# Product-key choices that read their scores from PSUM, one step sooner, with the turns of x at other steps

## The reference, cut to what matters

```python
q = (xb @ wq).reshape(PEER_BLOCK, PEER_HEADS, 2, D_KEY_HALF)
s1 = jnp.einsum('thd,hnd->thn', q[:, :, 0], keys1)
s2 = jnp.einsum('thd,hnd->thn', q[:, :, 1], keys2)
v1, i1 = lax.top_k(s1, PEER_TOPK)
v2, i2 = lax.top_k(s2, PEER_TOPK)
cand = (v1[..., :, None] + v2[..., None, :]).reshape(...)
cidx = (i1[..., :, None] * N_KEYS + i2[..., None, :]).reshape(...)
top_s, sel = lax.top_k(cand, PEER_TOPK)
eidx = jnp.take_along_axis(cidx, sel, axis=-1)
gate = jax.nn.softmax(top_s.astype(jnp.float32), axis=-1).astype(xb.dtype)
act = jax.nn.gelu(jnp.einsum('td,thkd->thk', xb, u_tab[eidx]))
return jnp.einsum('thk,thkd->td', gate * act, v_tab[eidx])
```

## Time and profile before

| | |
|---|---|
| median of three runs | 3038.26 us (3035.58 to 3039.6) |
| the profiled execution's own time | 3035.47 us |
| its span in the profile | 3033.6 us |
| mean granted TensorE clock | 0.846 of 2.4 GHz |
| busy: TensorE, VectorE, ScalarE, GpSimd | 2303.3, 2067.1, 2044.8, 1228.0 us |
| bytes moved, mean | 1226.64 MB, 404 GB/s |
| of these by the gathers' queue | 1107.36 MB, 88.6% of the DMA engines' span |

### The profile page before, as it was taken

How to read it: one execution, slowest core, us unless ns; L and a number is a source line. 1 busy time by engine, 2 the same in 40 slices (tenths; PEclk the granted TensorE clock), 3 DMA queues, 4 the chain that set the end, 5 groups by cost and what they waited for, 6 DMA issues and landing times.

```text
span 3033.6 us, 36636 instructions
## 1 busy us (share of the span) xinstructions
PE 2303.3 (76%) x12800; PEld 1880.0 (62%) x12800; DVE 2067.1 (68%) x5112; ACT 2044.8 (67%) x3704; POOL 1228.0 (40%) x1060
## 2 busy tenths in 40 slices
PE   9976887787668887877777877888777766667666
PEld 7765776665557766656566665665556555555555
DVE  2466887566688775666888744566588899955454
ACT  1277666668677566776677666667767777676666
POOL 0133333334333333444443344433344445456653
PEclk9987989998889889987887998989888886666666
DMA  7599999999999999999999999999999999999998
GB/s 301 190 416 397 413 408 414 419 420 413 420 421 409 420 417 415 420 404 420 420 416 406 404 422 419 419 419 396 405 420 420 418 418 409 415 418 419 422 420 333
DMA packets 180568, 1226.64 MB, mean 404 GB/s; under 512 B 20736, under 2 KB 21952, under 8 KB 40736
## 3 DMA queue, kind: packets, MB, share of 16 engines
q0 software_dynamic: 152064, 1107.36, 88.6%
q1 hardware_dynamic: 28032, 116.88, 9.6%
q10 hardware_dynamic: 288, 0.07, 0.0%
HBM read 1219.37 MB, written 4.86 MB: 404 GB/s over the span
## 4 chain that ended last, share of the span: by engine, by line
DMA 35%; DVE 24%; PE 22%; ACT 13%; issue 5%; POOL 1%; DVEq 0%; POOLq 0%; ACTq 0%
DMA ring<-in_uv,idx 35%; DVE ring L1459 12%; PE expert_sum L1116 8%; ACT ring L873 5%; PE mm L914 4%; PE x_ps L976 3%; ACT weights L869 2%; PE mm L1038 2%; PE mm L923 2%; ACT L860 1%; DVE pairs_left L1306 1%; ACT dots L860 1%; DVE pairs_left L1394 1%; DVE top_i L1315 1%; DVE pick_f L1400 1%
## 5 line engine op out<-in xcount | busy, mean ns | idle before, releaser
L661 POOL DMA_INDIRECT ring<-in_uv,idx x1056 | 1227.7, 1163 | 1781.8 <-PE expert_sum L1116 1574.7
L1116 PE MATMUL expert_sum<-ident_sb,ring 128*128 128x128 f32 x8448 | 1367.1, 317 | 581.3 <-ACT ring L873 579.8
L1459 DVE CUSTOM_DVE_ANT_0 ring<-ring,xn 128x1024 f32<-128x1024 f32 x1056 | 1286.7, 1223 | 737.8 <-DMA ring<-in_uv,idx 730.2
L1116 PEld LDWEIGHTS expert_sum<-ident_sb,ring 128*128 128x128 f32 x8448 | 1150.5, 165 | 838.6 <-ACT ring L873 767.9
L873 ACT ACTIVATE ring<-ring,weights 128x1024 f32<-128x1024 f32 x1056 | 1213.2, 1149 | 34.3
L860 ACT ACTIVATE dots<-dots 128x1 f32<-128x1 f32 x1056 | 211.5, 200 | 771.6 <-DVE dots L1459 768.2
L869 ACT ACTIVATE weights<-dots,gate 128x1 f32<-128x1 f32 x1056 | 311.1, 295 | 38.2
L914 PE MATMUL mm<-stream,xn_in 128*128 128x256 f32 (+1 forms) x912 | 258.4, 421 | 71.9 <-ACT qkvg L708 56.3
L1038 PE MATMUL mm<-turn,stream 128*128 128x256 f32 (+2 forms) x1024 | 278.4, 401 | 2.8 <-DVE xn_in L1155 2.8
L914 PEld LDWEIGHTS mm<-stream,xn_in 128*128 128x128 f32 (+1 forms) x912 | 166.9, 199 | 113.7 <-ACT qkvg L708 66.0
L923 PE MATMUL mm<-xn_in,stream 128*128 128x256 f32 (+1 forms) x640 | 183.7, 426 | 34.8 <-ACT conv_tmp L699 22.6
(11 more groups left out here) (233 smaller groups left out, 1517.4 us busy)
## 6 DMA issues: line engine op xcount, KB each, us to landing
stream<-in_wq SPq DMA_DIRECT2D x36, 1024.0 KB, 12.0
stream<-in_w_ret SPq DMA_DIRECT2D x26, 1024.0 KB, 9.4
stream<-in_w_conv SPq DMA_DIRECT2D x24, 1024.0 KB, 11.9
ring<-in_uv,idx POOLq DMA_INDIRECT x1056, 12.3
ring<-in_w_ret SPq DMA_DIRECT2D x7, 1024.0 KB, 12.4
x<-in_x SPq DMA_DIRECT2D x8, 512.0 KB, 8.7
w_out_sb<-in_w_out SPq DMA_DIRECT2D x1, 4096.0 KB, 28.9
out_y<-xn SPq DMA_DIRECT2D x8, 512.0 KB, 11.9
```

The costliest lines, as they stand in the source:

```text
L661: pool.indirect_dma_start(ring[:, g % RING, :], None, uv, bass.IndirectOffsetOnAxis(ap=rows, axis=0)).then_inc(landed[g % RING], 16)
L1116: ins = pe.matmul(expert_sum[:, c * P:(c + 1) * P], ring[:, g % RING, D + c * P:D + (c + 1) * P], ident_sb[:, :], is_transpose=True, start ...
L1459: dve.tensor_tensor_reduce(u, u, xn[:, t % 3, :], 1.0, 0.0, ALU.mult, ALU.add, dots[:, g % RING:g % RING + 1]).then_inc(dotted, 1)
```

## The change

The copies of the prompt tiles' scores to SBUF are taken out, with the tensor `scores`. VectorE's choice reads the scores in `tp`, and waits for TensorE's products (`keyed`) in place of the copies. Only the sample tile's scores are still copied, at the slot at which tile 7's scores of the same head would have been. `choose_at` is one slot sooner for every choice but one: head 1 of tile 0 stays at slot 0. `scores_left_tp` waits until VectorE has read the scores (`scores_read`, counted after the second half's MATCH_REPLACE8) and the sample's are copied. The turns of x move: tile 3 from slot 58 to 61, tile 5 from 274 to 277, sample from 526 to 528, tile 6 from 530 to 531, tile 7 from 534 to 537.

```diff
@@ x_turn_at
-    return first_use_at(group_of(t)) - 10 + 4 * place(t)
+    if group_of(t) == len(GROUPS) - 1:
+        return first_use_at(group_of(t)) + [-8, -5, 1][place(t)]
+    return first_use_at(group_of(t)) - 10 + 7 * place(t)
@@ choose_at
-    return choose_at(PH - 1, t - 1) + 7 * (h + 1) if t == SAMPLE else scores_at(h, t) + 1
+    return choose_at(PH - 1, t - 1) + 7 * (h + 1) if t == SAMPLE else scores_at(h, t)
@@ layer_kernel
-        scores = sb("scores", [P, 2, NK])
...
             if t < SAMPLE:
-                return scores[:, :, :]
+                return tp[:, score(h, t) % 2, 0:2 * NK].rearrange("p (s k) -> p s k", s=2)
@@ score_copies (ScalarE)
-                    if c == 0:
+                    if t < SAMPLE:
                         continue
                     n = rows_of(t)
-                    yield scores_at(h, t)
+                    yield scores_at(h, t - 1)
                     act.wait_ge(keyed, c)
-                    if t < SAMPLE:
-                        wait(act, scores_read, pick(h, t) - 1)
@@ scores_left_tp (TensorE)
                 if n:
                     pe.wait_ge(first_read, 2)
-                wait(pe, keyed_copied, n - 1)
+                sample = sum(t == SAMPLE for _, t in SCORES[:n])
+                wait(pe, scores_read, n - 1 - sample)
+                wait(pe, keyed_copied, sample)
@@ choices (VectorE)
-                            if s == 0:
-                                dve.wait_ge(keyed_copied, c)
+                            if s == 0 and t < SAMPLE:
+                                dve.wait_ge(keyed, c)
+                            elif s == 0:
+                                dve.wait_ge(keyed_copied, h + 1)
```

## The result

The changed kernel takes 3042.64 us (median of 10 runs, 3035.08 to 3049.46), the kernel before 3036.84 us (10 runs): a ratio of 1.0019, with a 95% interval of 1.0011 to 1.0027. A second set gave 3041.14 against 3037.37 us, 1.0013 (1.0003 to 1.0022). It is slower by 4 to 6 us: at the edge of what was called 0.2%, but a ratio of 1 lies outside both intervals. The time lies inside the stated range, and its direction is wrong: a gain of 0.9 us was forecast.

What follows compares the result with a forecast made beforehand. The gathers' DMA bytes were taken to bound the kernel. Terms of -1.4 (waits), 0 (indices), 0 (PSUM reads) and +0.5 us (turns) summed to -0.9, so 3038.26 us became 3037.4, range 3030 to 3044 us.

Steps and rivals of the forecast that it cites:

- The bound: Long plain stretch: the gathers' bytes set the pace, DMA share 1.01, about 2.5 us a slot, no compute engine full.
- The copies and the waits for them: ScalarE's 63 score copies: removal worth 0; VectorE's 52.2 us of waits for them: gain 1.4 us, between 0 and 4.2.
- Each choice starts one slot sooner: VectorE's choices, with exponential and gates, come one slot sooner; one worse wait, at slot 34, at most 0.4 us, taken as 0.
- rival (c): Tiles 0 and 1: VectorE blocks before unwritten scores, 14 waits, 35 us, a third may pass: +12 us, 3050 us; chance 0.08.
- The 3%: Share of a stall reaching the DMA engines, about 3%, read from GpSimd's late gathers near 442 and 909 us.
- The turns of x: Moved turns meet scores due at TensorE: 7.8 us more waiting, 0.2 us at 3%, taken as 0.5 us lost.
- Reading PSUM: VectorE's 378 reads of scores from PSUM: 6 ns more each, 2.3 us under DMA time, counted as 0.
- The earlier indices: GpSimd's one wait for a choice's indices in the loop, 3.46 us, mostly goes, worth 0.
- The signs: Observations set as proof of being right, among them VectorE's L1303 wait below 20 us and dips summing to 5 to 8 us.
- The sign set for being wrong: A DMA loss of over 2 us at slots 50 to 100, or in the 20 us after a moved turn.

Runs made afterwards that it cites:

- all choices late: Changed kernel with every choice one slot later, where it was before the change: 3036.78 us against 3036.82 for the kernel before, ratio 1.0004.
- turns alone: Kernel before with only the turns of x moved as in the change, copies and choices kept: 3043.12 us against 3036.82, ratio 1.0017.
- the scores sooner: Changed kernel with query passes of tiles 0, 1 and turns of tiles 2, 3 one slot sooner: 3039.65 us against 3037.37 for the kernel before, ratio 1.001.
- tiles 0 and 1 late: Changed kernel with only the choices of tiles 0 and 1 one slot later: 3038.77 us, ratio 1.0004 to the kernel before.

## Why the prediction was wrong, point by point

- **The bound.** Right: the DMA share is 1.01 in plain stretches in both kernels, and no engine became the bound.
- **The copies and the waits for them.** The sign was right and the size too small. 1.4 us was taken, between 0 and 4.2; all choices late against turns alone says -6.3 us by the medians and -3.9 by the ratios. So the upper bound was too low or just reached; it counted only what windows of 20 us lacked in DMA share.
- **"Each choice starts one slot sooner", at no price.** This is the step that failed. It was costed at nothing because a wait of VectorE passes on 3%, and for only one choice was a wait foreseen, at slot 34 (it came: 3.46 us). The same arithmetic (is TensorE's product there when VectorE reaches it?) was not made for the twelve choices from slot 51 on. The earlier trace rows was read as ScalarE's lateness, TensorE having "long been done". That is so at slot 52, but not everywhere: the copies' own row has 10.0 us of idle time that ended with TensorE's scores. One such copy, behind VectorE's wait of 3.21 us at slot 87 of the kernel before:

```profile
384.75 0.38 ACT L806 ACTIVATE scores<-tp 128x256 f32<-128x256 f32 x1 [3.22 <-PE tp L1066]
```

  In the busy stretch of tiles 0 and 1 TensorE is up to three slots late, and the copy's slot was part of the margin that hid it. Measured: 24.7 us more waits by the means in slots 30 to 130 (28.2 to 31.0 against 3.9 to 7.0), and 4.2 us (medians) to 6.0 us (rows) more time. This is rival (c), which was given 35 us of waits, a third passed on and a chance of 0.08; its waits are the ones that the runs show, at half its price or less. That the loss comes with the early choices of tiles 0 and 1 is shown; that it comes through their waits alone is not, by the run with the scores sooner.
- **The 3%.** It was taken from two gaps of GpSimd which fell, by the prediction's own argument, when other transfers filled the DMA engines, and used as a rule. If the waits of tiles 0 and 1 are the whole cause, the runs give a sixth to a quarter for waits that follow each other every seven slots (4.2 to 6.0 of 24.7 us); and a stretch with a stall of 14.54 us and two smaller gaps grew by 11.0 us.
- **The turns of x.** 0.5 us was taken of 7.8. Measured +6.3 us with copies (2.9 for tile 3's, 3.2 for the others), and by the medians 3.8 for the others without copies. So this term was too small as well. But the forecast waits don't explain it. In the profile after, TensorE waits 0.84 us before tile 5's score at 278 and not at all before the one at 539, where 4.1 and 3.6 us were forecast. In the run with the turns alone, which has the loss, they are 2.75 and 0.51 us; with all choices late, which has no loss, the first is 4.60 us and the second isn't there. The two rows at slot 278:

```profile
936.19 1.15 PE L1068 MATMUL tp<-keys_sb,qT 128*128 128x128 f32 x4 [2.75 <-issue]
```

```profile
932.33 0.98 PE L1068 MATMUL tp<-keys_sb,qT 128*128 128x128 f32 x3 [4.60 <-issue]
```

  Which wait makes the moved turns dearer is open. One thing that the profile shows is argued only: ScalarE's part of the norm, with its two table loads, has moved with the turn, and TensorE waits 4.57 us for ScalarE at 928.67. Against it: with tiles 0 and 1 late the same wait lasts 4.58 us, in a kernel without a clear loss.
- **Reading PSUM.** Right: MATCH_REPLACE8 takes 280 ns from tp against 276, and FIND_INDEX8 291 (lines below). The measured 4 to 6 ns decide against the 65 ns more that were worked out from the page of the Trainium skill (Perfetto Trace Analysis, Optimizing Scalar/DVE Operations).
- **The earlier indices.** Right: GpSimd's wait for the indices of gather 32, 3.46 us, is gone. The profile after puts one other wait down to indices, 2.69 us at 399.44 before gather 96. The indices written just before it are those of a choice of tile 1, which that gather doesn't use, so the name of that wait isn't its cause.
- **The signs.** VectorE's wait at the choices was to fall below 20 us and is 36.8; the dips were to sum to 5 to 8 us and sum to 11.6. The sign set for being wrong, over 2 us of DMA time lost at slots 50 to 100, was just reached (2.0 us in the window at 300, around slot 61) and not passed, so it was set too high for a loss that is spread.

The tile view of tp in the changed kernel (duration min/median/max in ns):

```profile
L1305 DVE MAX8 top_v<-tp x126: 279/295/300, 127.8 to 2512.3; 128x8 f32<-128x128 f32 x126
...
L1307 DVE FIND_INDEX8 top_i<-top_v,tp x126: 289/291/293, 128.2 to 2512.7; 128x8 uint32<-128x128 f32 x126
...
L1308 DVE MATCH_REPLACE8 pairs_left<-top_v,tp x126: 278/280/284, 128.5 to 2513.0; 128x128 f32<-128x128 f32 x126
```

In all, by the medians and in this order: moved turns +6.3, reading from PSUM -6.3, early choices +4.8 (the mean of the two sets, against all choices late). By the ratios and the other pairs of runs they are 5 to 6, 4 to 6 and 3 to 5 us. They were forecast as +0.5, -1.4 and 0. The sizes are those of this order of steps; another was measured only in part (the turns other than tile 3's cost 3.8 us by the medians without the copies, 3.2 with them).

## What to carry to other kernels

When a copy between two engines is taken out, look at how late the producer is in each stretch, and not only at how late the copier was: the copy's step may be the margin that covers the producer, and a consumer that works in order then blocks its own main work in front of it. Here the early choices with two slots behind their scores (tiles 2 to 7) cost nothing that could be measured, and those with one slot (tiles 0 and 1 from slot 51 on) came with a loss of 3 to 5 us. And don't turn one observed gap into a rate for how much of a stall reaches the bounding resource: measure a stall where nothing else fills in. Where a change has several parts, as here, run each alone: two of them cost and one gained, and the sum hid that.

## What the hardware showed that was not expected

The DMA share doesn't see all that is lost. Slots 32 to 160, changed kernel and the one with tiles 0 and 1 late (stretches):

```profile
219.00:608.50 389.50, 304.21 (x1808) 264.10 (x1807) 282.66 (x772) 263.36 (x470) 146.47 (x130) 0.89 1.00 406
```

```profile
219.20:601.20 382.00, 298.81 (x1793) 260.24 (x1792) 282.90 (x773) 263.94 (x471) 143.21 (x129) 0.90 1.01 414
```

Both carry the same bytes, 158 MB. The changed kernel takes 2.0% longer and moves 2.0% less in a microsecond, but its share is only about 1% lower. So about half of the loss is idle time of the DMA engines, and the other half is a lower rate while they count as busy.

In slots 64 to 96 the share doesn't show the loss at all:

```profile
316.00:410.60 94.60, 80.81 (x477) 70.77 (x475) 76.16 (x231) 60.00 (x111) 35.12 (x34) 0.93 1.01 412
```

```profile
312.50:404.20 91.70, 79.22 (x482) 70.10 (x481) 77.21 (x232) 60.71 (x112) 36.39 (x33) 0.93 1.01 418
```

The share is 1.01 in both, with 412 GB/s against 418 and 2.9 us between them. Some 1.3 us of that is the lower rate; the rest is bytes, 39.0 MB against 38.3, since a stretch also holds transfers of the slots around it. Why the rate falls is open; that fewer gathers were queued was not measured. The GB/s column over a long stretch, or the times of the slots themselves, show the loss; the sum of the dips in the share does not.
